# FFN loop of a decoder layer: two tiles for weight sums instead of three, six raw weight tiles instead of five, three sums begun later

## The reference

```
hf = _rms_norm(x, ffn_norm_g[l])
x = x + (jax.nn.silu(hf @ w_ffn_gate[l]) * (hf @ w_ffn_up[l])) @ w_ffn_down[l]
```

## Time and profile before

| | us |
|---|---|
| median of 3 runs | 1637.94 (1637.84 to 1639.34) |
| profiled execution, its own time | 1638.1 |
| its span in the profile | 1636.3 |
| TensorE (PE) busy | 1628.2, 7412 matmuls |
| VectorE (DVE) busy | 1183.0 |
| ScalarE (ACT) busy | 884.2 |
| FFN rounds 1 to 10 | about 986 to 1608 |

### The profile page before, as it was taken

One profiled execution on the slowest core, in us unless ns is written; L12 is line 12 of the kernel. 1 busy time (PEld: TensorE's weight loads), 2 busy tenths in 40 slices (PEclk: granted clock), 3 DMA queues, 4 the chain that ended last, 5 costly groups with the idle time before them and its releaser, 6 DMA issues.

```text
span 1636.3 us, 20500 instructions
## 1 busy us (share of the span) xinstructions
PE 1628.2 (100%) x7412; PEld 1345.8 (82%) x7412; DVE 1183.0 (72%) x1201; ACT 884.2 (54%) x964; POOL 79.7 (5%) x73
## 2 busy tenths in 40 slices
PE   9999999999999999999999999999999999999999
PEld 7888888888888888888888887888888888888887
DVE  5565544554577767655565579999999999999995
ACT  6654544444555554444444564665665666656653
POOL 0000000000011100000000000100100100100101
PEclk9999999999999999999999999999999999999999
DMA  9876556566555555576655566868868868868866
GB/s 335 282 208 193 172 161 181 170 194 191 174 168 166 158 177 167 182 234 193 194 179 186 183 223 203 243 208 252 248 211 249 246 218 243 245 218 246 251 211 177
DMA packets 178002, 341.30 MB, mean 209 GB/s; under 512 B 11792, under 2 KB 16400, under 8 KB 177168
## 3 DMA queue, kind: packets, MB, share of 16 engines
q1 hardware_dynamic: 167056, 319.45, 60.4%
q0 software_dynamic: 10880, 20.97, 7.0%
HBM read 317.31 MB, written 2.10 MB: 195 GB/s over the span
## 4 chain that ended last, share of the span: by engine, by line
PE 97%; DVE 2%; DMA 0%; ACT 0%; issue 0%; SPq 0%; DVEq 0%
PE acc L1284 56%; PE at L1499 8%; PE at L1500 8%; PE at L1501 8%; PE acc L1500 4%; PE acc L1501 4%; PE acc L1499 4%; PE at L1306 2%; DVE sum_rest L1170 1%; PE at L1359 0%; PE at L1344 0%; DMA raw<-in_w_mem_kv 0%; DVE f_raw_rest L1164 0%; DVE sum L1184 0%; ACT f_hi L716 0%
## 5 line engine op out<-in xcount | busy, mean ns | idle before, releaser
L784 DVE TENSOR_TENSOR w_lo<-raw,w_hi 128x1024 fp32r<-128x1024 f32 x332 | 402.8, 1224 | 344.5 <-ACT w_hi L428 342.5
L428 ACT ACTIVATE w_hi<-raw 128x1024 fp32r<-128x1024 f32 x332 | 351.4, 1061 | 424.2 <-PE acc L1284 402.4
L1284 PE MATMUL acc<-w_hi,hT_hi 128*128 128x512 f32 x896 | 354.1, 395 | 0.1
L1284 PE MATMUL acc<-w_hi,hT_lo 128*128 128x512 f32 x896 | 349.1, 390 | 0.0
L1284 PE MATMUL acc<-w_lo,hT_hi 128*128 128x512 f32 x896 | 348.9, 389 | 0.0
L1284 PEld LDWEIGHTS acc<-w_hi,hT_hi 128*128 128x128 f32 x896 | 168.3, 188 | 36.4 <-issue 1.3
L1284 PEld LDWEIGHTS acc<-w_hi,hT_lo 128*128 128x128 f32 x896 | 168.2, 188 | 35.5
L1284 PEld LDWEIGHTS acc<-w_lo,hT_hi 128*128 128x128 f32 x896 | 168.4, 188 | 33.9
L716 ACT ACTIVATE f_hi<-sum 128x2048 fp32r<-128x2048 f32 x60 | 115.3, 1922 | 124.1 <-DVE sum L1191 124.1
L1284 PE MATMUL acc<-w_hi,oT_hi 128*128 128x512 f32 x448 | 176.1, 393 | 1.8 <-DVE oT_lo L803 1.3
L1284 PE MATMUL acc<-w_hi,oT_lo 128*128 128x512 f32 x448 | 174.5, 390 | 0.0
(11 more groups left out here) (215 smaller groups left out, 2207.1 us busy)
## 6 DMA issues: line engine op xcount, KB each, us to landing
raw<-in_w_in SPq DMA_DIRECT2D x208, 512.0 KB, 4.1
f_raw<-in_w_ffn_down SPq DMA_DIRECT2D x88, 512.0 KB, 4.7
f_raw<-in_w_ffn_gate SPq DMA_DIRECT2D x80, 512.0 KB, 4.0
f_raw<-in_w_ffn_up SPq DMA_DIRECT2D x80, 512.0 KB, 5.1
proj<-down POOLq DMA_DIRECT2D x40, 512.0 KB, 6.3
raw<-in_w_mem_kv SPq DMA_DIRECT2D x32, 512.0 KB, 6.5
raw<-in_w_out SPq DMA_DIRECT2D x32, 512.0 KB, 3.6
raw<-in_w_o_mem SPq DMA_DIRECT2D x16, 512.0 KB, 4.7
```

Source lines behind the costliest of these rows:

```text
L428: act.activation(w_hi[:, s % RING], raw[:, s % RING], ACT.Copy).then_inc(hi_done, 1)
L784: v.tensor_tensor(w_lo[:, s % RING], raw[:, s % RING], w_hi[:, s % RING].bitcast(F32), ALU.subtract).then_inc(lo_done, 1)
L1284: e = pe.matmul(acc[p][:, t, :], a[:, k0 + k, tok], w[:, s % RING, k, :], start=first and k == 0 and n == 0, stop=last and k == 1 and n == 2)
```

## The change

Three edits that go together. `SUMS` becomes 2 and `RAWS` 6: the third sum tile's memory becomes the sixth raw tile. On VectorE, `sum_first` of sums 2, 4 and 5 moves behind the remainders of the pair before (S1, S3, S4), to stand directly ahead of its `sum_rest`. Two waits of the first round follow the new tiles: raw units 4 and 5 both wait for the last pair of the weight ring, and `sum_first` of sum 2 no longer does, as it now uses sum 0's tile.

```
-PARTS, UNITS, SLOTS, RAWS, SUMS, NS = 18, 12, 5, 5, 3, 6
+PARTS, UNITS, SLOTS, RAWS, SUMS, NS = 18, 12, 5, 6, 2, 6
...
-            ... ("f_raw4", quad_tile, F32), ("sum2", quad_tile, F32),
+            ... ("f_raw4", quad_tile, F32), ("f_raw5", quad_tile, F32),
...
                 if g >= RAWS:
                     sp.wait_ge(part_done, unit_part(g - RAWS) + 1)
                 elif g >= 3:
-                    sp.wait_ge(pair_used, G_F0 + (16 if g == 4 else 0))
+                    sp.wait_ge(pair_used, G_F0 + (16 if g >= 4 else 0))
...
                     v.wait_ge(part_done, part(e + 1, SUM_PART[j]) + 1)
-                elif i == 2:
-                    v.wait_ge(pair_used, G_F0 + 16)
...
-                sum_first(f, 2, 3)
                 low_three(f, S1W, 2, 1)
                 low_sums(f, S1T, 1)
+                sum_first(f, 2, 3)
                 sum_rest(f, 2, 3)
                 low_three(f, S2W, 3, 2)
                 low_sums(f, S2T, 2)
                 sum_first(f, 3, 5)
                 low_whole(f, N1, 4)
                 sum_rest(f, 3, 5)
-                sum_first(f, 4, 6)
                 low_three(f, S3W, 5, 3)
                 low_sums(f, S3T, 3)
+                sum_first(f, 4, 6)
                 sum_rest(f, 4, 6)
-                sum_first(f, 5, 7)
                 low_three(f, S4W, 6, 4)
                 low_sums(f, S4T, 4)
+                sum_first(f, 5, 7)
                 sum_rest(f, 5, 7)
                 low_three(f, S5W, 7, 5)
                 low_sums(f, S5T, 5)
```

More of the change, by code:

```diff
@@ L151, in program @@
             ("down0", [P, TB, NCOL], F32), ("down1", [P, TB, NCOL], F32),
-            ("f_hi3", quad_tile, F32R), ("f_hi4", quad_tile, F32R), ("f_raw4", quad_tile, F32), ("sum2", quad_tile, F32),
+            ("f_hi3", quad_tile, F32R), ("f_hi4", quad_tile, F32R), ("f_raw4", quad_tile, F32), ("f_raw5", quad_tile, F32),
             ("f_hi0", quad_tile, F32R), ("f_hi1", quad_tile, F32R), ("f_hi2", quad_tile, F32R), ("f_raw3", quad_tile, F32),
```

## The result

The changed kernel takes 1671.8 us (median of 4 runs, 1671.15 to 1672.55), the kernel before beside it 1637.89: 33.9 us more, a ratio of 1.0204 (95% interval 1.0192 to 1.0217). The forecast was 1670.6. The profiled execution took 1672.55 with a span of 1670.8.

The account below looks back on a forecast made before the run. TensorE, busy for all but 8 us, bounds the kernel, and VectorE has only some 3.5 us to spare a round. Nine rounds x 3.45 plus 1.61 in round 1 add 32.7 us: 1670.6 us, range 1667 to 1674.5.

Parts of the forecast that it names:

- The places of the stalls: TensorE stalls each round before S2T (0.45 us), N1 (0.62), S4T (0.24), S5W (1.66) and S5T (0.45).
- The short waits for ScalarE: VectorE's T remainders: S1T, S3T and S4T also show S2T's 0.19 us wait for ScalarE's copy; five a round, before two.
- The wait's end: VectorE at sum 2: can begin 0.27 us after TensorE ends S0T, having stood about 3.5 us, in rounds 2 to 10.
- The chain: VectorE's sequence from sum 2 to S5T's remainder: 6.87 + 8.95 + 6.87 + 6.95 = 29.64 us, then 0.06 to TensorE.
- A round: Rounds 2 to 10: S5T starts at 29.97 us behind S0T instead of 26.52, so each round is 3.45 us longer.
- No building up, and VectorE's rest ahead of L1195: Next S0T resets the sequence, so delays don't accumulate; VectorE's wait for TensorE's last sum product falls from 2.56 to some 0.8 us.
- Round 1: First FFN round: no wait at sum 2, but S5T starts at 1027.51 against 1025.90, 1.61 us later.
- The sixth raw tile at 0: Loads on SyncE may be issued one unit earlier; as no transfer is waited for, it gains 0.
- The cost of a direct wait: VectorE's sum_rest directly behind sum_first: rows differ by 0.13 us a wait from no wait, already inside the 29.64 us.
- The rival of the slack: VectorE's 2.56 us before its last sum wait pays for the stall; 0.9 us a round left, 1648 us; chance 0.03.
- Not slower: Wait at sum 2 turns out short, needing it to begin by 1058.50; 1637.3 to 1639.5 us; chance 0.02.
- The clock: Stalls up to 1.7 us bring TensorE to 1.2 GHz in every round; 5 us more a round, 1716 us; chance 0.04.

Follow-up runs that it names:

- wait_s0t: Kernel before with only the three sum_first moves, plus sum 2's sum_first waiting for S0T from round 2 on; 1672.04 us, ratio 1.0208.
- sum4_back: Changed kernel with sum_first of sum 4 alone back in its old place, ahead of S3W's remainder; 1666.37 us, ratio 1.0171 to the kernel before.
- two_sums_five_raws: Changed kernel with five raw tiles instead of six, the sixth's memory left unused; 1671.35 us, ratio 1.0202 to the kernel before.
- three lengths of wait: Kernel before with the three moves, sum 2's sum_first also waiting for S0W, S0T or S1W from round 2 on: 1647.62, 1672.04, 1690.53 us.
- moves_only: Kernel before with only its three sum_firsts moved, keeping three sum tiles and five raw tiles; 1640.02 us, ratio 1.0012.
- tiles_only: Changed kernel with the three sum_firsts back in their old places, so two sum tiles and six raw tiles; 1733.66 us, ratio 1.0583 to the kernel before.
- wait_s1w: Kernel before with the three moves, plus sum 2's sum_first waiting for S1W from round 2 on; 1690.53 us, ratio 1.0317.

## Why the prediction was right, point by point

- **The direction, and where it comes from**: right. wait_s0t reproduces the whole loss without touching a tile.
- **The places of the stalls**: right, all five. Measured in round 2 as the start of the part less the usual pitch, they are S2T 0.31, N1 0.46, S4T 0.08, S5W 1.53 and S5T 0.28 us, each 0.13 to 0.17 less than forecast: the wait ended 0.07 earlier, and part of the delay lies in slower pitches between the stalls (below).
- **The short waits for ScalarE**: one too many. Five a round were forecast, four came (41 in ten rounds): S1T, at 1059.01, waits for nothing. Its place is taken by S1W's remainder, which waits 0.22 us for its copy. Both lie ahead of S0T's end, so the chain does not see them.
- **The waits of sums 3, 4 and 5**: the prediction says nothing of them. They were met with 2 us or more to spare, so leaving them out cost nothing here, but it gave no reason for it.
- **The wait's end**: sized at 0.27 us behind S1W's first matmul, measured 0.20 (1064.50 to 1064.70). VectorE stood for 3.4 us, not 3.5.
- **The chain**: 29.64 forecast, 29.62 measured, with 6.87, 8.95, 6.87, 6.95 against 6.87, 8.94, 6.87, 6.94. The last step, 0.06 us to TensorE, is the same (1094.32 to 1094.38). S5T starts 29.88 us behind S0T's end, where 29.97 was forecast.
- **A round**: 3.45 forecast, 3.51 measured. S5T comes 29.88 − 26.52 = 3.36 late. The other 0.15 is a term that the sum left out: from S5T's start to the next round's first matmul behind the transposes the changed kernel takes 25.48 us (to 1119.86), the kernel before 25.32. A matmul behind a stall is followed after 0.34 us instead of 0.227, and some of those after it start 0.236 apart. That the period is right to 0.06 us is in part luck: S5T was put 0.09 us too late, and 0.15 was left out behind it.
- **No building up, and VectorE's rest ahead of L1195**: right; the periods stay within 65.63 and 65.68, the rest is 1.0 us where 0.8 was forecast.
- **Round 1**: +1.61 forecast; 63.24 − 61.64 = 1.60 measured.
- **The sum**: 9 x 3.51 + 1.60 = 33.2 us, against 32.7 forecast and 33.9 between the medians. The difference to the medians lies ahead of the loop. In the changed kernel's four runs two have a mean clock of 0.999 (1672.31 and 1672.55 us) and two of 1.000 (1671.15 and 1671.28). The profiled one is of the first kind; near its start a stretch shows the low level, which the kernel before's profile has not:

```profile
8.90:12.30 3.40, 3.40 (x10) 2.65 (x9) 2.39 (x4) 2.15 (x4) 0.00 (x0) 0.50 1.06 393
```

```profile
8.53 0.47 PE L1282 MATMUL acc<-w_hi,oT_hi 128*128 128x512 f32 x1 [1.99 <-DVE oT_lo L803]
```

  The kernel before at the same place:

```profile
8.00:12.00 4.00, 3.45 (x14) 2.61 (x15) 2.48 (x5) 1.98 (x4) 0.00 (x0) 1.00 1.05 389
```

  So its round 1 begins 1.24 us later (990.96 against 989.72), before any changed instruction of the FFN counts. The two other profiles with a low stretch there, sum4_back and two_sums_five_raws, begin round 1 at 991.02 and 991.00; the eight without one at 989.33 to 990.32.
- **The sixth raw tile at 0**: right (two_sums_five_raws).
- **The cost of a direct wait**: the three new ones show 0.03 us from a sum_first's end to its sum_rest (1064.70 + 1.22 to 1065.95), 1.25 as pitch, against 1.13 or 1.14 without a wait. The Trainium skill's "VectorE: DVE Perf Modes", "The DRAIN you can't avoid", measured with eight copies that a semaphore after each costs nothing extra. Here an instruction that waits for the one before it starts 0.12 us later behind it than one that does not, and going by the rows was right. The waiting ones also read what the one before wrote, so the rows don't tell the semaphore's part from the data's.
- **The rival of the slack**: wrong. It is refuted by the three lengths of wait, whose rounds grow one for one. The slack ahead of L1197 did pay for the moves (2.56 to 1.0 us in moves_only), but not for the wait.
- **Not slower**: its deciding point was a start of sum 2 3.45 us earlier, 0.13 us after VectorE is free for it. In moves_only sum 2 begins as soon as VectorE is free, and the period is 62.16 us: the condition was placed rightly, but two tiles do not meet it.
- **The clock**: did not come in the changed kernel's loop, whose longest idle time is 1.36 us. It came where idle times were longer: in tiles_only, 2.99 us, behind both long stalls of every round from the second on, but in round 1, where TensorE stood 2.98 us twice, only behind the second; in wait_s1w, 1.90 us, in three of nine rounds, though all nine have that same idle time ahead of S2W. Two of the three stretches, and below them the idle time of round 2, which the clock did not follow, are

```profile
1274.20:1277.60 3.40, 3.40 (x9) 2.62 (x9) 3.40 (x3) 3.04 (x2) 0.00 (x0) 0.50 0.01 4
1342.50:1345.90 3.40, 3.40 (x9) 2.62 (x8) 3.40 (x3) 2.50 (x2) 0.00 (x0) 0.50 0.00 0
```

```profile
1070.70 0.50 PE L1501 MATMUL at<-f_hi,hT_hi 128*128 128x512 f32 x1 [1.90 <-DVE f_raw_rest L1164]
```

  I gave it 0.04 at 5 us a round. No run bears that price out: the low stretches shown here are 3.4 us long, and where the clock did fall in the loop it cost 0.5 to 0.7 us a round (tiles_only) or nothing (wait_s1w). The reason given against it, the row of 1.29 us at 8.08, was a thin one: at the same place in the changed kernel's own profile TensorE stood for 1.99 us and the clock did fall. What the profiles do show is that the loop's longest idle time, 1.36 us, is shorter than any that a fall of the clock followed. The Trainium skill's "TensorE: Matmul & The Clock Gate", "A second HAM failure mode: psum-queue depth-cycling", tells of a kernel whose clock swung from short, frequent idles; with five stalls a round, the longest 1.36 us idle, this loop shows no such swing.

## What to carry to other kernels

A tile's rotation is a wait in disguise: with N tiles, use k waits for the end of use k − N. Before taking a tile away, find that use in the consumer's order, and add to its end the producer's whole chain up to the next part that is due; the difference to that due time is nearly the cost per round (3.36 of 3.51 us here), and the producer's average idle time says little about it. Work that is moved out of the time in which it covered a copy is free while the producer has time, and costs that cover once it has none: see rounds 2 to 10 of moves_only, and the 0.53 us of sum4_back.

## What the runs showed of the hardware that was not expected

- The low clock level can cost far less than its length. In wait_s1w, rounds with a stretch of 3.4 us at 1.2 GHz are no longer than the others (67.73, 67.74 and 67.72 against 67.73 to 67.80): TensorE was ahead of VectorE's chain there, and the slow matmuls only filled what would have been the next stalls: the gap before S5W is 1.42 us in these rounds and 1.75 in the others.
- A pause of TensorE is followed by a second small loss, 0.11 us to the second matmul and a few pitches of 0.236, some 0.15 us from S5T on in each round.
- Some executions start with a stretch at the low level and some don't, worth 1.2 us in 1671. In the eleven profiles it goes with how long TensorE stood before its first weight product, at about 8 us: 1.84, 1.99 and 2.26 us in the three that have the stretch, 0.80 to 1.72 us in the eight that don't. That time differs from run to run with nothing changed in this part of the kernel. It fits the two groups of the changed kernel's four runs, and the kernel before beside moves_only: its two runs with a mean clock of 0.999 took 1638.97 and 1639.30 us, its other thirteen 1637.69 to 1638.52. What makes TensorE stand longer there in some executions is not known.
